# A transformer kernel on one core: the first two weight units in halves, the first two input tiles one by one

## What is computed

```python
def rms_norm(x, g):
    xf = x.astype(jnp.float32)
    y = xf * lax.rsqrt(jnp.mean(xf * xf, axis=-1, keepdims=True) + EPS)
    return (y * g.astype(jnp.float32)).astype(x.dtype)

def swiglu(h, w_gate, w_up, w_down):
    return (jax.nn.silu(h @ w_gate) * (h @ w_up)) @ w_down

x = x + 0.5 * swiglu(rms_norm(x, ffn1_norm[i]), ffn1_w_gate[i], ffn1_w_up[i], ffn1_w_down[i])
```

## Time and profile before

| | |
|---|---|
| median of 3 runs | 1680.75 us (1680.71 to 1680.81) |
| profiled execution | 1680.63 us |
| its span, first to last instruction | 1678.8 us |
| instructions | 21140 |
| busy share of the span | PE 100%, DVE 61%, ACT 38%, POOL 42% |
| moved by DMA | 173.14 MB, mean 103 GB/s |

### The profile page before, as it was taken

One profiled execution on the slowest core, in us unless ns is written; L12 is line 12 of the kernel. 1 busy time (PEld: TensorE's weight loads), 2 busy tenths in 40 slices (PEclk: granted clock), 3 DMA queues, 4 the chain that ended last, 5 costly groups with the idle time before them and its releaser, 6 DMA issues.

```text
span 1678.8 us, 21140 instructions
## 1 busy us (share of the span) xinstructions
PE 1671.5 (100%) x7672; PEld 1367.4 (81%) x7672; DVE 1021.2 (61%) x1205; ACT 638.5 (38%) x895; POOL 713.1 (42%) x303
## 2 busy tenths in 40 slices
PE   9999999999999999999999999999999999999999
PEld 7887888887788888888888888888877768888887
DVE  7767566527565446357665566775574753969451
ACT  5222222226665656321322322213446754333321
POOL 2444344434343421444444344444356533444443
PEclk9999999999999999999999999999999999999999
DMA  5332233325411220342423323332252033233243
GB/s 199 100 110 91 79 100 100 101 88 198 136 64 62 89 76 26 100 133 94 141 93 106 102 89 100 102 102 91 93 189 76 26 113 113 90 99 100 92 143 118
DMA packets 44193, 173.14 MB, mean 103 GB/s; under 512 B 5034, under 2 KB 5418, under 8 KB 42829
## 3 DMA queue, kind: packets, MB, share of 16 engines
q1 hardware_dynamic: 39024, 148.13, 26.9%
q10 hardware_dynamic: 5084, 23.82, 4.2%
HBM read 159.22 MB, written 10.62 MB: 101 GB/s over the span
## 4 chain that ended last, share of the span: by engine, by line
PE 96%; DVE 2%; ACT 1%; issue 0%; DMA 0%; POOL 0%; SPq 0%; DVEq 0%; ACTq 0%; POOLq 0%
PE psum L339 27%; PE psum L340 27%; PE psum L344 26%; PE psum L331 1%; PE psum L1279 1%; PE psum L333 1%; PE psum L332 1%; PE psum L1851 1%; PE psum L388 1%; PE psum L383 1%; PE psum L384 1%; PE psum L1828 1%; PE psum L1269 1%; PE psum L819 1%; DVE spec_out L2466 1%; PE psum L1297 1%
## 5 line engine op out<-in xcount | busy, mean ns | idle before, releaser
L274 POOL TENSOR_TENSOR wlo<-raw,whi 128x1024 fp32r<-128x1024 f32 (+2 forms) x256 | 657.7, 2569 | 870.1 <-ACT whi L319 869.6
L319 ACT ACTIVATE whi<-raw 128x1024 fp32r<-128x1024 f32 (+2 forms) x259 | 286.1, 1105 | 698.4 <-PE psum L344 665.1
L339 PE MATMUL psum<-h_hi,whi 128*128 128x512 f32 x1336 | 528.2, 395 | 1.5 <-DVE spec_out L2466 0.8
L340 PE MATMUL psum<-h_lo,whi 128*128 128x512 f32 x1336 | 520.4, 390 | 0.0
L344 PE MATMUL psum<-h_hi,wlo 128*128 128x512 f32 x1336 | 337.0, 389 | 0.0
L339 PEld LDWEIGHTS psum<-h_hi,whi 128*128 128x128 f32 x1336 | 250.9, 188 | 59.8 <-issue 5.9
L340 PEld LDWEIGHTS psum<-h_lo,whi 128*128 128x128 f32 x1336 | 251.0, 188 | 53.3 <-issue 2.6
L344 PEld LDWEIGHTS psum<-h_hi,wlo 128*128 128x128 f32 x1336 | 250.8, 188 | 52.5 <-POOL wlo L274 0.4
L339 PE MATMUL psum<-mid_hi,whi 128*128 128x512 f32 x352 | 137.2, 390 | 0.0
L340 PE MATMUL psum<-mid_lo,whi 128*128 128x512 f32 x352 | 137.0, 389 | 0.0
L709 DVE TENSOR_TENSOR silu<-sig,gate 128x512 f32<-128x512 f32 x44 | 100.3, 2279 | 41.8 <-ACT sig L654 41.8
(11 more groups left out here) (407 smaller groups left out, 2380.2 us busy)
## 6 DMA issues: line engine op xcount, KB each, us to landing
raw<-wk_dram SPq DMA_DIRECT2D x220, 512.0 KB, 3.5
raw<-wd_dram SPq DMA_DIRECT2D x32, 704.0 KB, 4.1
raw<-wp_dram SPq DMA_DIRECT2D x8, 640.0 KB, 3.9
x_scratch<-xT ACTq DMA_DIRECT2D x2, 2048.0 KB, 8.1
spectra_scratch<-spec_out ACTq DMA_DIRECT2D x4, 1024.0 KB, 5.5
xT<-x_scratch ACTq DMA_DIRECT2D x8, 512.0 KB, 4.3
spec<-spectra_scratch ACTq DMA_DIRECT2D x2, 2048.0 KB, 10.1
xT<-x_dram SPq DMA_DIRECT2D x4, 512.0 KB, 7.6
```

The costliest lines, as they stand in the source:

```text
L274: pool.tensor_tensor(wlo[s][:, 0:w], raw[s][:, 0:w], whi[s][:, 0:w].bitcast(F32), ALU.subtract).then_inc(lo_ready, 1)
L319: act.activation(whi[s][:, 0:w], raw[s][:, 0:w], ACT.Copy).then_inc(hi_ready, 1)
L339: pe.matmul(dst, a, m_hi[:, c, :], start=start and c == chunks[0][0], stop=False)
L340: pe.matmul(dst, a, m_lo[:, c, :], start=False, stop=False)
```

## The change

Units 0 and 1 are loaded and split in halves of four chunks. First come the first halves (split by ScalarE and VectorE, counted on gained_hi and gained among the gained tiles), the second halves follow after input tile 3 (counted on hi_ready and lo_ready, as the whole units were). Input tiles 0 and 1 are loaded one by one. PE's products are put in the order in which the parts are made; FIRST_READY gives for each input tile the count on the shared semaphores. The zero matmuls go from 8 to 5. Some semaphores are merged (the vectors share one with the first half, the rope tables share const_landed, input tile 1 shares x_moved with the stores of x), and the counts waited for are raised to fit.

```diff
-        x_stored = sem("x_stored")
-        vec_landed = sem("vec_landed")
+        x_moved = sem("x_moved")
+        half_landed = [sem("vec_and_first_half_landed"), sem("second_unit_half_landed")]
...
+        FIRST_READY = (2, 3, 5, 6, 7, 8, 9, 10)
...
-                for _ in range(8):
+                for _ in range(5):
                     pe.matmul(bank(7, 256), idle_zeros[:, 0:P], idle_zeros[:, P:P + 256], start=True, stop=True)
...
+                pe.wait_ge(gained_hi, FIRST_READY[0])
+                on_high(0, 0, hi)
+                pe.wait_ge(gained, 1)
+                on_high(0, 0, lo)
+                pe.wait_ge(gained_hi, FIRST_READY[1])
+                on_high(0, 1, hi)
+                on_high(0, 1, lo)
                 for k in range(2):
-                    pe.wait_ge(gained_hi, k + 1)
-                    on_high(0, k, hi)
-                pe.wait_ge(lo_ready, 1)
-                for k in range(2):
-                    on_high(0, k, lo)
-                    pe.wait_ge(gained, k + 1)
+                    pe.wait_ge(gained, FIRST_READY[k])
                     on_low(0, k)
-                pe.wait_ge(hi_ready, 2)
+                pe.wait_ge(gained_hi, 4)
                 for k in range(2):
                     on_high(1, k, hi)
                     on_low(1, k)
-                pe.wait_ge(gained_hi, 3)
-                on_high(0, 2, hi)
-                on_high(0, 2, lo)
-                pe.wait_ge(lo_ready, 2)
+                pe.wait_ge(gained, 4)
                 for k in range(2):
                     on_high(1, k, lo)
                 for k in range(2, DT):
-                    pe.wait_ge(gained_hi, k + 1)
-                    for g in range(1 if k == 2 else 0, 2):
+                    pe.wait_ge(gained_hi, FIRST_READY[k])
+                    for g in range(2):
+                        if k == 4:
+                            pe.wait_ge(hi_ready, g + 1)
                         on_high(g, k, hi)
+                    for g in range(2):
+                        if k == 4:
+                            pe.wait_ge(lo_ready, g + 1)
                         on_high(g, k, lo)
-                    pe.wait_ge(gained, k + 1)
+                    pe.wait_ge(gained, FIRST_READY[k])
...
         @block.sync
-            load_unit(sp, 0, 0, "k", 0)
-            for i in range(4):
-                sp.dma_start(xT[:, 2 * i:2 * i + 2, :], x_in[:, 2 * i:2 * i + 2, :]).then_inc(x_landed[i], 16)
-                if i == 0:
-                    load_unit(sp, 1, 0, "k", 1)
+            def load_half(u, g, signal):
+                cols = slice(g * D // 2, (g + 1) * D // 2)
+                sp.dma_start(raw[u][:, cols], wk[u][:, cols]).then_inc(signal, 16)
+
+            def load_x(first, last, signal):
+                sp.dma_start(xT[:, first:last, :], x_in[:, first:last, :]).then_inc(signal, 16)
+
+            load_half(0, 0, half_landed[0])
+            load_x(0, 1, x_landed[0])
+            load_x(1, 2, x_moved)
+            load_half(1, 0, half_landed[1])
+            load_x(2, 4, x_landed[1])
+            load_half(0, 1, landed[0])
+            load_half(1, 1, landed[1])
+            load_x(4, 6, x_landed[2])
+            load_x(6, 8, x_landed[3])
             sp.dma_start(constf[:, :, :], constf_in).then_inc(const_landed, 16)
             stream_loads(sp)
...
         @block.scalar
-            act.dma_start(vec[:, 0:NVEC], vec_in).then_inc(vec_landed, 16)
-            act.wait_ge(landed[0], 16)
-            act.activation(first_hi[:, :], raw[0][:, 0:D], ACT.Copy).then_inc(hi_ready, 1)
-            next_hi[0] = 1
-            act.wait_ge(vec_landed, 16)
+            def half_hi(u, g):
+                cols = slice(g * D // 2, (g + 1) * D // 2)
+                act.wait_ge(landed[u] if g else half_landed[u], 16 if g or u else 32)
+                act.activation((first_hi, whi[1])[u][:, cols], raw[u][:, cols],
+                               ACT.Copy).then_inc(hi_ready if g else gained_hi, 1)
+
+            act.dma_start(vec[:, 0:NVEC], vec_in).then_inc(half_landed[0], 16)
+            half_hi(0, 0)
             for k in range(DT):
...
                 act.activation(h_hi[:, k, :], xT[:, k, :], ACT.Copy, scale=col("ffn1_norm", k)).then_inc(gained_hi, 1)
                 if k == 1:
-                    split_hi_to(act, 2)
+                    half_hi(1, 0)
+                elif k == 3:
+                    half_hi(0, 1)
+                    half_hi(1, 1)
+                    next_hi[0] = 2
             split_hi_to(act, 3)
...
         @block.vector
-            dve.wait_ge(vec_landed, 16)
-            dve.wait_ge(hi_ready, 1)
-            dve.tensor_tensor(first_lo[:, :], raw[0][:, 0:D], first_hi[:, :].bitcast(F32),
-                              ALU.subtract).then_inc(lo_ready, 1)
+            def half_lo(u, g):
...
+                dve.tensor_tensor((first_lo, wlo[1])[u][:, cols], raw[u][:, cols], hi.bitcast(F32),
+                                  ALU.subtract).then_inc(lo_ready if g else gained, 1)
+
+            dve.wait_ge(half_landed[0], 32)
+            half_lo(0, 0)
             for k in range(DT):
-                dve.wait_ge(gained_hi, k + 1)
+                dve.wait_ge(gained_hi, FIRST_READY[k])
                 dve.scalar_tensor_tensor(h_lo[:, k, :], xT[:, k, :], col("ffn1_norm", k), h_hi[:, k, :].bitcast(F32),
                                          ALU.mult, ALU.subtract).then_inc(gained, 1)
                 if k == 1:
-                    dve.wait_ge(hi_ready, 2)
-                    dve.tensor_tensor(wlo[1][:, 0:D], raw[1][:, 0:D], whi[1][:, 0:D].bitcast(F32),
-                                      ALU.subtract).then_inc(lo_ready, 1)
+                    half_lo(1, 0)
+                elif k == 3:
+                    half_lo(0, 1)
+                    half_lo(1, 1)
```

More of the change, by code:

```diff
@@ L1548, in vector_gate @@
                 if b == 0:
-                    dve.wait_ge(x_stored, 16)
+                    dve.wait_ge(x_moved, 32)
                 dve.tensor_copy(xT[:, b, :], bank(7)).then_inc(self.seven_read, 1)
@@ L1713, in load @@
             def load(self, act):
-                act.dma_start(rope[:, :], rope_in).then_inc(rope_landed, 16)
+                act.dma_start(rope[:, :], rope_in).then_inc(const_landed, 16)
                 for a, b, n in ((0, 96, 32), (32, 64, 32), (64, 0, 64)):
-                    act.dma_start(rope_odd[a:a + n, :], rope_in[b:b + n, :]).then_inc(rope_landed, 16)
+                    act.dma_start(rope_odd[a:a + n, :], rope_in[b:b + n, :]).then_inc(const_landed, 16)
             def tensor_latents(self, pe):
@@ L2024, in scalar_copy @@
                 if h == 0 and s == 0:
-                    act.wait_ge(x_stored, 32)
+                    act.wait_ge(x_moved, 48)
                 act.activation(self.turned_probs(h, s), bank(6), ACT.Copy).then_inc(self.copied0, 1)
@@ L2186, in vector_copy @@
                 if h == 0 and s == 1:
-                    dve.wait_ge(x_stored, 32)
+                    dve.wait_ge(x_moved, 48)
                 dve.tensor_copy(self.turned_probs(h, s), bank(7)).then_inc(self.copied1, 1)
@@ L2995, in _ @@
         def _(act):
-            act.dma_start(vec[:, 0:NVEC], vec_in).then_inc(vec_landed, 16)
-            act.wait_ge(landed[0], 16)
-            act.activation(first_hi[:, :], raw[0][:, 0:D], ACT.Copy).then_inc(hi_ready, 1)
-            next_hi[0] = 1
-            act.wait_ge(vec_landed, 16)
+            def half_hi(u, g):
[5 more added lines that the diff above has]
+            half_hi(0, 0)
             for k in range(DT):
-                act.wait_ge(x_landed[k // 2], 16)
+                if k < 2:
+                    act.wait_ge(x_moved if k else x_landed[0], 16)
+                else:
+                    act.wait_ge(x_landed[k // 2], 16)
                 act.activation(h_hi[:, k, :], xT[:, k, :], ACT.Copy, scale=col("ffn1_norm", k)).then_inc(gained_hi, 1)
                 if k == 1:
-                    split_hi_to(act, 2)
+                    half_hi(1, 0)
[3 more added lines that the diff above has]
+                    next_hi[0] = 2
             split_hi_to(act, 3)
@@ L3016, in _ @@
             act.wait_ge(x_updated, XS["out1"])
-            act.dma_start(x_dram, xT[:, :, :]).then_inc(x_stored, 16)
+            act.dma_start(x_dram, xT[:, :, :]).then_inc(x_moved, 16)
             foxp.scalar(act)
@@ L3042, in _ @@
             clear_sum(dve)
-            dve.wait_ge(vec_landed, 16)
-            dve.wait_ge(hi_ready, 1)
-            dve.tensor_tensor(first_lo[:, :], raw[0][:, 0:D], first_hi[:, :].bitcast(F32),
-                              ALU.subtract).then_inc(lo_ready, 1)
+            def half_lo(u, g):
+                cols = slice(g * D // 2, (g + 1) * D // 2)
+                if g:
+                    dve.wait_ge(hi_ready, u + 1)
+                else:
+                    dve.wait_ge(gained_hi, 4 if u else 1)
+                hi = (first_hi, whi[1])[u][:, cols]
```

(8 more changed lines are left out.)

7 lines of the change are left out of this document (3 added, 4 removed).

## The result

| | before | after |
|---|---|---|
| median of 7 runs | 1680.80 us (1680.71 to 1681.23) | 1686.96 us (1685.83 to 1687.79) |
| ratio after to before | | 1.0036 (95% interval 1.0026 to 1.0045) |
| profiled execution | 1680.63 us | 1687.42 us |
| its span | 1678.8 us | 1685.6 us |

The changed kernel is slower by 6.2 us, where +2.9 was forecast and 1685.8 was the top of the range. The runs before lie within 0.5 us, those after within 2.0.

A forecast was written before the change was run, and what follows sets the result against it. PE bounds the kernel, but VectorE's sums set L453: a late unit 2 and a sum held by POOL delay it 3.0 us, less 0.1 of existing idle. With +2.9 the forecast was 1683.6 us, range 1681.2 to 1685.8.

The forecast's parts named there:

- VectorE's sums set L453: At L453 in unit 3: PE waits for the eighth sum, so its early start gains nothing unless sums come earlier.
- POOL's unit 4 then catches a sum: Last three sums: POOL starts near 24.15 and holds one; sums end at 28.7, L453 starts 3.0 us later.
- C: At L453: no sum held, only unit 2 late; +0.8 us, 1681.5; chance 0.12.
- D: At L453: the sums do not bind and PE keeps its lead; -1.6 us, 1679.1; chance 0.1.
- E: At the start: PE still starts at 7.5, unit 2 late all the same; +2.9 us, counted within the forecast's 0.58.
- the first data: Start: first half split at 4.7, tile 0 ready at 5.9, PE starting near 6.0 instead of 7.5.
- what is moved behind: Unit 2's transfer, waiting for lo_ready 1: issued at 11.05, split at 14.7 instead of 13.84, 0.85 us late.
- B: From L453: the clock falls to 1.2 GHz in PE's new stall; 1 to 2.4 us more, about 1685.5; chance 0.2.
- 1.6 us ahead at the first L339: After PE's first 48 products: the next unit's first product comes at about 17.3 instead of 18.9.
- Cost nothing: Start: five idle products for eight leave PE idle at most some 0.3 us before 6.0, at no cost.

The follow-up runs named there:

- b_late_unit2: Kernel before, with the stream of units (unit 2 first) issued only once input tile 3's low part is made; 1686.09 us, ratio 1.0031.
- a_poolwait: Changed kernel, with POOL's unit 4 waiting until the eighth sum is done; 1684.46 us, ratio 1.0020.
- a_ownraw: Changed kernel, with units 0 and 1 in buffers of their own, so units 2 and 3 are issued right behind the constants; 1686.01 us.
- b_small: Kernel before, with units 0 and 1 transferred in two column halves each and tiles 0 and 1 one by one, old order; 1681.30 us.
- a_warm: Changed kernel, with 12 matmuls of zeros in front of the norm's matmul (L453); 1685.93 us, ratio 1.0029.
- b_idle5: Kernel before, with five matmuls of zeros for eight at the start; 1682.01 us, ratio 1.0007.
- b_norm6: Kernel before, with the norm's matmul behind six chunks of unit 3 instead of two; 1680.53 us, ratio 0.9999.
- a_own_pool_norm6: Changed kernel, units 0 and 1 in own buffers, POOL's unit 4 behind the eighth sum, norm's matmul behind six chunks of unit 3; 1679.90 us.

## Why the prediction was wrong

**Right.** That VectorE's sums set L453 and PE's early start is worth nothing there: PE was 1.9 us ahead at its first product, and b_late_unit2 loses 5.4 us without any lead. That lo_ready 1, moved behind four gained tiles, makes unit 2 late. That POOL's unit 4 then catches a sum: forecast in place and mechanism, measured at 1.80 us (a_poolwait takes the held sum away). The side, slower. C and D fell: one sum was held, and L453 was late, not early. E did not come: the vectors landed 3.1 us after their issue (3.9 was taken), and PE started at 5.58, sooner than the forecast's 6.0. The fit of the Trainium skill that the prediction cites for the first data (DMA: Bandwidth & Descriptors, "Anatomy of one DMA") is given for transfers that GpSimd issues, and these are SP's; here a half unit landed 2.8 us after its issue and a whole one, before, 3.8.

**The term of the sum that was mis-sized: the step "what is moved behind".** I had unit 2 issued at 11.05, landing 3.65 us later, split at 14.7, at worst 1.5 late. It was issued at 11.74, landed 4.8 later and was split at 16.58, 2.74 late. Two things were missing.
- *The issue, 0.7 us.* I let the first data come in at the old pace. Tile 3's high part was forecast near 9.4 and ended at 10.13 (8.79 + 1.34), with ScalarE idle for tiles 1 and 2 before it, and lo_ready 1 moved with it.
- *The landing, 1.15 us.* The text said that all ahead of unit 2 would have arrived by 12.4, "so the queue is no hindrance", and took the landing of 3.5 to 3.8. That 12.4 was read from the old queue. In the new one the constants landed only at 13.9. In the profiles of six kernels with this start they landed at 13.4 to 14.1, unit 2 4.1 to 5.5 us after its issue, and it was split at 15.5 to 17.6; in b_late_unit2, with the old queue, 3.5 us. Unit 3's transfer close behind is not the reason, since b_late_unit2 has it too.

Why the new queue is slower to empty is open in part. It carries the same bytes in more and smaller transfers, and 217 GB/s came between 4 and 6 us for 315; without any wait (a_ownraw) unit 2 is still split at 15.11. b_small points the same way, but moved ScalarE's table load as well.

This term moved the sum by 1.9 us. With 16.58 in it the fifth sum ends at 23.26 + 2.74 = 26.0. POOL's unit 4, forecast from PE's lead at 24.15, could not start before POOL's own unit 3 was done near 25.2, which the text had not reckoned with, and started at 25.34; from there the forecast's rule (a held sum ends 0.55 behind POOL) gives 28.05 + 0.55 = 28.6 for the held one and 30.2 for the last: the trace to a tenth.

**The step left to a rival: the clock.** The text forecast 4.5 us of idle and in the same breath 0.58 for a clock that stays up, because no row of before showed a fall. The price given for B, 1 to 2.4 us, held (2.25 here, 1.59 in b_late_unit2, 1.58 in a_ownraw), the chance of 0.2 did not: it belonged to the forecast. a_warm, in which the clock stays at 1.00 with PE kept busy, shows that the idle brought it down. The rule of the Trainium skill cited for B (TensorE: Matmul & The Clock Gate, Part 1: the clock falls back after idle) agrees with the trace. With 16.58 for unit 2 and the fall in the sum it comes to 2.74 + 1.80 + 2.25, the measured 6.79.

**A smaller miss without effect.** PE was to be 1.6 us ahead at the first L339 and was 0.55, since it stood 1.17 us for tile 1. The text said that the size of the lead does not matter, and b_late_unit2 with none bears that out. "Cost nothing" for five idle products in place of eight holds for the changed kernel's trace, where the products from 7.82 on are 0.23 us apart; in the kernel before it did cost some 1.3 us in most runs (b_idle5).

## What to carry to other kernels

Before making the start of a stream faster, find the first place at which the stream meets another engine's result, and ask what sets that result. Here it was a chain of eight sums that hangs on one transfer, and the edit that let PE start 1.9 us earlier made that transfer's data 2.7 us late. When a semaphore that also releases a buffer is signalled later, price the transfer behind it with its queue as it will then be, and where the forecast holds a stall of several microseconds on TensorE, put the lower clock behind it into the sum, not among the rivals.

## What the runs showed that I had not expected

- With the first units and tiles in transfers with rows of 2 KB the queue brought 259 GB/s between 4 and 6 us (b_small), with rows of 4 KB 315; in the changed kernel 217. One execution each.
- With a second wait added in front of ScalarE's first instruction, its table load of 1.28 us started at 4.65 instead of 1.20 and lay on the chain that ended last (b_small).
- With the constants landed at 12.5, unit 2's transfer, issued at 12.06, landed after 3.5 us with another issued right behind it; with the constants landed at 13.9 it took 4.8 from 11.74.
- The clock fell around a gap in which PE stood 3.4 to 4.3 us (the profiles of five kernels) and stayed up in a_poolwait's profile with 2.3 us. Eight of a_poolwait's ten runs have 0.999 on record all the same; how long PE stood in them is not known. What the fall costs was 1.6 to 2.3 us in the three profiles in which PE stood at the norm's matmul.
- The spread of the runs does not follow the stall alone: 1.4 to 2.9 us with one, 0.31 in b_norm6 without, but 2.2 in a_own_pool_norm6, which has none either.
